# Twelve pairs of weight units as seven block products each, the memory branch moved ahead, and weight sums on VectorE

## What is computed

```python
proj = h @ w_in
(q_lat, kv_lat, k_pe, c_b, c_c, c_u, q_mem,
 g_attn, g_conv, g_mem, r) = split_cols(proj, IN_SIZES)
...
o_conv = c_b * centred_short_conv(c_c * c_u, conv_w, conv_b) * jax.nn.silu(g_conv)
...
r_attn, r_conv, r_mem = split_cols(jax.nn.sigmoid(r + b_gate), (D_MODEL, D_MODEL, D_MODEL))
y = r_attn * (o_attn @ w_br_attn) + r_conv * (o_conv @ w_br_conv) + r_mem * (o_mem @ w_br_mem)
return x + y @ w_out
```

## Time and profile before

| | |
|---|---|
| Median of 3 runs | 2596.67 us (2593.72 to 2598.73) |
| Profiled execution, first to last instruction | 2595.3 us |
| Mean granted TensorE clock | 0.986 |
| TensorE busy | 2476.7 us, 95% |
| VectorE busy | 1323.2 us, 51% |
| ScalarE busy | 762.5 us, 29% |
| GpSimd busy | 875.1 us, 34% |

### The profile page before, as it was taken

How to read it: one execution, slowest core, us unless ns; L and a number is a source line. 1 busy time by engine, 2 the same in 40 slices (tenths; PEclk the granted TensorE clock), 3 DMA queues, 4 the chain that set the end, 5 groups by cost and what they waited for, 6 DMA issues and landing times.

```text
span 2595.3 us, 33878 instructions
## 1 busy us (share of the span) xinstructions
PE 2476.7 (95%) x13700; PEld 2026.8 (78%) x13700; DVE 1323.2 (51%) x1338; ACT 762.5 (29%) x1166; POOL 875.1 (34%) x383
## 2 busy tenths in 40 slices
PE   6999888899999999999999799999999999999999
PEld 3788677677888888888877588878888877878877
DVE  3799678737654444444575887731022321342341
ACT  4201267614221211211344477720000110242010
POOL 1443300043444444444433200043344334513442
PEclk9999899999999999999999899999999999999999
DMA  6111456311111111111121400011111111113112
GB/s 261 41 41 57 116 174 185 125 49 39 43 55 43 51 47 48 48 48 48 49 110 65 136 1 2 2 41 49 65 49 49 49 41 57 57 33 121 46 45 89
DMA packets 57528, 173.79 MB, mean 67 GB/s; under 512 B 5748, under 2 KB 24440, under 8 KB 55992
## 3 DMA queue, kind: packets, MB, share of 16 engines
q1 hardware_dynamic: 51712, 149.13, 17.5%
q10 hardware_dynamic: 5688, 22.81, 2.3%
HBM read 161.37 MB, written 10.56 MB: 66 GB/s over the span
## 4 chain that ended last, share of the span: by engine, by line
PE 85%; DVE 7%; ACT 3%; issue 2%; DMA 1%; POOL 1%; SPq 0%; ACTq 0%; DVEq 0%; POOLq 0%
PE region L277 25%; PE region L279 25%; PE region L278 25%; PE pv L1936 2%; PE aux L1926 2%; DVE conv L1141 1%; ACT na_prob L1025 1%; DMA x_sb<-x_t 1%; DVE na_prob L1066 1%; PE region L2218 1%; PE pv L835 1%; PE pv L985 1%; DVE q_h L1841 1%; DVE q_h L1847 1%; DVE head_scale L421 1%
## 5 line engine op out<-in xcount | busy, mean ns | idle before, releaser
L2354 POOL TENSOR_TENSOR w_hi<-w_raw,der 128x1024 fp32r<-128x1024 f32 x186 | 362.6, 1949 | 1508.8 <-PE region L279 1464.4
L277 PE MATMUL region<-h_hi,w_hi 128*128 128x512 f32 x1760 | 691.6, 393 | 13.3 <-POOL w_lo L2357 4.9
L278 PE MATMUL region<-h_lo,w_hi 128*128 128x512 f32 x1760 | 687.8, 391 | 0.0
L279 PE MATMUL region<-h_hi,w_lo 128*128 128x512 f32 x1760 | 687.5, 391 | 0.0
L2357 POOL TENSOR_TENSOR w_lo<-w_raw,w_hi 128x1024 fp32r<-128x1024 f32 x186 | 505.0, 2715 | 14.6
L277 PEld LDWEIGHTS region<-h_hi,w_hi 128*128 128x128 f32 x1760 | 332.3, 189 | 91.8 <-issue 9.8
L279 PEld LDWEIGHTS region<-h_hi,w_lo 128*128 128x128 f32 x1760 | 332.1, 189 | 69.8
L278 PEld LDWEIGHTS region<-h_lo,w_hi 128*128 128x128 f32 x1760 | 332.3, 189 | 68.0
L277 PE MATMUL region<-ff_hi,w_hi 128*128 128x512 f32 x512 | 199.2, 389 | 0.0
L278 PE MATMUL region<-ff_lo,w_hi 128*128 128x512 f32 x512 | 199.2, 389 | 0.0
L279 PE MATMUL region<-ff_hi,w_lo 128*128 128x512 f32 x512 | 199.2, 389 | 0.0
(11 more groups left out here) (358 smaller groups left out, 3807.0 us busy)
## 6 DMA issues: line engine op xcount, KB each, us to landing
w_raw<-units SPq DMA_DIRECT2D x186, 512.0 KB, 3.3
w_raw<-w_ada_late SPq DMA_DIRECT2D x32, 512.0 KB, 4.3
bias<-na_bias SPq DMA_DIRECT2D x24, 384.0 KB, 3.7
...
head_wide<-v_spill SPq DMA_DIRECT2D x16, 512.0 KB, 3.8
...
x<-x_t ACTq DMA_DIRECT2D x1, 4096.0 KB, 14.8
```

Of the source, the lines that this page charges most:

```text
L277: pe.matmul(dst, wh, xh, start=first, stop=False)
L278: pe.matmul(dst, wh, xl, start=False, stop=False)
L279: return pe.matmul(dst, wl, xh, start=False, stop=last)
L2354: pool.tensor_tensor(w_hi[:, s], w_raw[:, s], one_col.broadcast_to([P, 1024]), ALU.mult)\
```

## The change

**Seven products.** Two units (a pair) are the rows of a 2 x 2 block matrix: a11 and a12 are the first and second half of the inputs of one tile of outputs, a21 and a22 of the other. The tokens' halves and the inputs' halves make the 2 x 2 blocks of `h2` (near is tokens 0 to 511, far the rest). Eight block products of 12 matmuls become seven (Strassen in Winograd's form), each with its own 512-wide chunk of weights: a11, a21+a22-a11, a21, a11-a21, a12, a12-(a21+a22-a11), a22. The pairs are the 16 units of `cv` and the two gates of each group of `br1`. Four chunk slots lie in `w_hi` and `w_lo`. ScalarE now writes a chunk's high part (`highs_act`), GpSimd its low part (`chunks_pool`), VectorE the four sums of weights (`sums_dve`) and five sums of results in PSUM (`pair_dve`). Three banks serve a pair, so product 4 (j == 3) waits for the first sum of results.

**Blocks of h2.** Three combinations of blocks are stored beside `h2` (`far_dve`, `far_act`, behind each group of `br0`), and `last_far_dve` writes a fourth in place over `h2`'s far half once branch 0 has read it.

**Order.** The memory stages and branch 2 come directly behind `mla`, then `gattn`, branch 0, `cv`, branch 1, `out2`. The memory rows' squares are added up on GpSimd and summed by one matmul; the memory heads are four queries and then four keys. `x3` is loaded behind branch 1's last pair and scaled during `out2`, whose units GpSimd splits from the last `chunk_done` on.

```diff
-               ("uq", 4), ("uk", 3), ("uv", 1), ("gattn", 4), ("br0", 12), ("cv", 16), ("br1", 12),
-               ("mkq", 8), ("mv", 4), ("gmem", 4), ("br2", 12), ("out2", 8)]
+               ("uq", 4), ("uk", 3), ("uv", 1), ("mkq", 8), ("mv", 4), ("gmem", 4), ("br2", 12),
+               ("gattn", 4), ("br0", 12), ("cv", 16), ("br1", 12), ("out2", 8)]
...
+    def far_dve(e, ch, k):
+        near, far = slice(0, HALF), slice(HALF, T)
+
+        def whole(slot, kk, t):
+            ch(e.tensor_tensor(far_f32[:, slot], h2_hi[:, kk, t].bitcast(F32), h2_lo[:, kk, t].bitcast(F32), ALU.add))
+
+        def made(slot, a, b):
+            e.tensor_tensor(far_f32[:, slot], far_f32[:, a], far_f32[:, b], ALU.subtract).then_inc(sem("far_made"), 1)
+
+        whole(0, k, far)
+        whole(1, k, near)
+        made(1, 0, 1)
+        whole(2, 4 + k, far)
+        made(0, 2, 0)
+        reach(e, "far_made", 3 * k + 2)
+        made(2, 2, 1)
+        for n, (which, slot) in enumerate(FAR_ORDER):
+            reach(e, "far_hi", 3 * k + n + 1)
+            e.tensor_tensor(far_lo[which][:, k], far_f32[:, slot], far_hi[which][:, k].bitcast(F32), ALU.subtract)\
+                .then_inc(sem("far_lo"), 1)
+        reach(e, "far_lo", 3 * k + 3)
...
+    def last_far_dve(e, ch):
+        near, far = slice(0, HALF), slice(HALF, T)
+
+        def low(k):
+            reach(e, "far_hi", 12 + k + 1)
+            e.tensor_tensor(h2_lo[:, k, far], far_f32[:, 2 * (k % 2)], h2_hi[:, k, far].bitcast(F32), ALU.subtract)\
+                .then_inc(sem("far_lo"), 1)
+
+        e.wait_ge(unit_done, UNIT0["br0"] + 11)
+        for k in range(4):
+            a = 2 * (k % 2)
+            if k >= 2:
+                reach(e, "far_lo", 12 + k - 1)
+            ch(e.tensor_tensor(far_f32[:, a], h2_hi[:, 4 + k, near].bitcast(F32), h2_lo[:, 4 + k, near].bitcast(F32), ALU.add))
+            ch(e.tensor_tensor(far_f32[:, a + 1], far_hi[1][:, k].bitcast(F32), far_lo[1][:, k].bitcast(F32), ALU.add))
+            e.tensor_tensor(far_f32[:, a], far_f32[:, a], far_f32[:, a + 1], ALU.subtract).then_inc(sem("far_made"), 1)
+            if k:
+                low(k - 1)
+        low(3)
+        reach(e, "far_lo", 16)
...
+    SIDES = [(h2_hi[:, 0:4, near_x], h2_lo[:, 0:4, near_x]), (far_hi[1], far_lo[1]), (far_hi[0], far_lo[0]), (far_hi[2], far_lo[2]),
+             (h2_hi[:, 4:8, near_x], h2_lo[:, 4:8, near_x]), (h2_hi[:, 4:8, far_x], h2_lo[:, 4:8, far_x]),
+             (h2_hi[:, 0:4, far_x], h2_lo[:, 0:4, far_x])]
+    BANK = [0, 1, 2, 1, 0, 2, 1]
+
+    def pair_pe(e, pair):
+        for j in range(7):
+            e.wait_ge(chunk_ready, pair.done(j))
+            if j == 0 and pair.before is not None:
+                e.wait_ge(second_sum, pairs[pair.before].summed(5))
+                e.wait_ge(near_end, pair.before + 1)
+            if j == 3:
+                e.wait_ge(second_sum, pair.summed(1))
+            if j == 4:
+                e.wait_ge(first_copy, pair.n + 1)
+            if j == 5:
+                e.wait_ge(second_sum, pair.summed(3))
+            if j == 6:
+                e.wait_ge(second_sum, pair.summed(2))
+            at, s, cols = chunk_of(pair.c + j)
+            wh, wl = w_hi[at, s, cols], w_lo[at, s, cols]
+            xh, xl = SIDES[j]
+            dst = pair.banks[BANK[j]]
+            for k in range(4):
+                w = slice(k * P, k * P + P)
+                e.matmul(dst, wh[:, w], xh[:, k], start=(j < 3 and k == 0), stop=False, skip_group_check=True)
+                e.matmul(dst, wh[:, w], xl[:, k], start=False, stop=False, skip_group_check=True)
+                last = e.matmul(dst, wl[:, w], xh[:, k], start=False, stop=(k == 3), skip_group_check=True)
+            last.then_inc(chunk_done, 1)
+
+    def part_pe(e, pos, c):
...
+        def high(upto):
+            while high.next < min(upto, N_CHUNKS):
+                c = next(at)
+                high.next = c + 1
+                src, step, u = sources[c]
+                if c < 4:
+                    e.wait_ge(unit_done, UNIT0["cv"] - 1 + c // 2)
                 else:
...
+                    e.wait_ge(chunk_done, c - 3)
+                e.wait_ge(raw_loaded[u % 2], 16 * (u // 2 + 1))
+                if step:
+                    reach(e, "w_sum", step)
+                copy(e, w_hi[chunk_of(c)], src).then_inc(sem("chunk_hi"), 1)
...
+    def chunks_pool(e):
+        def low(c, src):
+            reach(e, "chunk_hi", c + 1)
+            e.tensor_tensor(w_lo[chunk_of(c)], src, w_hi[chunk_of(c)].bitcast(F32), ALU.subtract).then_inc(chunk_ready, 1)
...
+            low(c, a11)
+            reach(e, "w_sum", n + 3)
+            low(c + 1, a11)
+            low(c + 2, a21)
+            reach(e, "w_sum", n + 4)
+            low(c + 3, w_diff[:])
+            low(c + 4, a12)
+            low(c + 5, a11)
+            freed(c + 5)
+            low(c + 6, a22)
+            freed(c + 6)
...
+        if i == 0:
+            e.wait_ge(raw_loaded[s], 16 * (pair.unit // 2 + 1))
+            e.wait_ge(raw_loaded[1 - s], 16 * ((pair.unit + 1) // 2 + 1))
+            if pair.n:
+                e.wait_ge(chunk_ready, pairs[pair.n - 1].done(3))
+            combine(1, w_diff[:], a11, a21, ALU.subtract)
+            combine(2, a21, a21, a22, ALU.add)
+        elif i == 1:
+            e.wait_ge(chunk_ready, c + 1)
+            combine(3, a11, a21, a11, ALU.subtract)
+        else:
+            e.wait_ge(chunk_ready, c + 2)
+            combine(4, a11, a12, a11, ALU.subtract)
...
+        a, b, c = pair.banks
+        e.wait_ge(first_copy, pair.n + 1)
+        e.wait_ge(chunk_done, pair.done(1))
+        add(1, second_t, first_copy_t, b)
+        e.wait_ge(chunk_done, pair.done(3))
+        add(2, third_t, first_copy_t, b)
+        far_far(lambda dst: add(3, dst, third_t, c))
+        if ahead:
+            sums_dve(e, ahead, 0)
+        e.wait_ge(chunk_done, pair.done(5))
+        near_far(lambda dst: add(4, dst, second_t, c))
+        if ahead:
+            sums_dve(e, ahead, 1)
+        e.wait_ge(chunk_done, pair.done(6))
+        far_near(lambda dst: add(5, dst, first_copy_t, b))
+        if ahead:
+            sums_dve(e, ahead, 2)
...
+        reach(e, "far_lo", 16)
+        for n in range(8):
+            if n == 1:
+                wait_region(e, pos.use)
+                wait_region(e, pos.use + 1)
+            pair_pe(e, pairs[n])
...
+    def last_branch_dve(e, pos, ch):
+        for p in range(4):
+            pair = pairs[8 + p]
+            if p:
+                reach(e, "br1_used", 2 * p)
+                for i in range(3):
+                    sums_dve(e, pair, i)
+            pair_dve(e, pair, lambda add: add(tmp[:, 1, far_t]), lambda add: add(tmp[:, 1, near_t]),
+                     lambda add: add(tmp[:, 0, far_t]))
+            for dd in range(2):
+                use, d = pos.next_use(), 2 * p + dd
+                e.wait_ge(near_end, pair.n + 1)
+                reach(e, "gate_half", 3 * p + 2 + dd)
+                e.wait_ge(chunk_done, parts[p] + dd + 1)
+                e.tensor_tensor(tmp[:, dd], region[:, use % 2], tmp[:, dd], ALU.mult).then_inc(free[use % 2], 1)
+                e.wait_ge(free[use % 2], use // 2 + 1)
+                e.tensor_tensor(y[:, d], y[:, d], tmp[:, dd], ALU.add).then_inc(sem("br1_used"), 1)
...
+            split_range(UNIT0["mkq"], UNIT0["cv"])
+            chunks_pool(pool)
+            pool.wait_ge(chunk_done, N_CHUNKS)
+            split_range(UNIT0["out2"], N_UNITS, CHUNK_UNITS)
...
+            branch_dve(dve, pos, ch, 0, behind=lambda p: far_dve(dve, ch, p))
+            last_far_dve(dve, ch)
+            for i in range(3):
+                sums_dve(dve, pairs[0], i)
+            meet(dve, pos, 3)
+            cv_dve(dve, pos, ch)
+            meet(dve, pos, 3)
+            last_branch_dve(dve, pos, ch)
             out2_dve(dve, pos, ch)
 
...
+            mem_sums_pe(pe)
+            tell()
+            mem_heads.pe(pe, pos, meanwhile=lambda: mv_pe(pe, pos))
+            tell()
+            ended(3)
+            mem_att.pe(pe, pos)
+            tell()
+            reach(pe, "ma_stored", MH * TT)
+            gate_pe(pe, pos, "gm", "gmem", o_mem)
+            tell()
+            branch_pe(pe, pos, 2, "gm_lo")
```

More of the change, by code:

```diff
@@ L2100, in branch_act, with branch_dve @@
             pos.next_use(), pos.next_use()
-    def branch_dve(e, pos, ch, b, ahead=None):
+            if behind:
+                behind(p)
+    def branch_dve(e, pos, ch, b, first=False, behind=None):
         u0 = UNIT0[f"br{b}"]
@@ new lines, in far_act @@
+    def far_act(e, k):
+        for n, (which, slot) in enumerate(FAR_ORDER):
+            reach(e, "far_made", 3 * k + n + 1)
+            copy(e, far_hi[which][:, k], far_f32[:, slot]).then_inc(sem("far_hi"), 1)
+    def last_far_dve(e, ch):
[16 more added lines that the diff above has]
+        reach(e, "far_lo", 16)
@@ new lines, in part_pe @@
+    def part_pe(e, pos, c):
+        use = pos.next_use()
```

(35 more changed lines are left out.)

364 lines of the change are left out of this document (237 added, 127 removed).

## The result

| | before | changed |
|---|---|---|
| median of 4 runs each | 2596.94 us | **2630.23 us** |
| lowest to highest | 2593.72 to 2598.73 | 2626.49 to 2632.28 |
| span of the profiled execution | 2595.3 | 2628.0 |
| mean granted clock | 0.986 | 0.975 |

The changed kernel is slower: ratio 1.0124 [1.011, 1.0137], 33 us. I had forecast 2618, in a range of 2597 to 2636.

A forecast was written before the change was run, and what follows sets the result against it. TensorE, busy 95% of the span, was taken as the bound. Costs of 65.4 us against savings of 44.2 gave +21.2, so 2618 us from a median of 2596.67; own range 2606 to 2629, overall 2597 to 2636.

The forecast's parts named there:

- five drops: +8.5: After long new TensorE waits: five falls to the 1.2 GHz level, about 1.7 us each, +8.5 us (1.7 to 17).
- Rival 1: Every wait over 2 us brings a clock drop, twelve or more: +21 instead of 8.5, about 2631 us; chance 0.15.
- Rival 4: Products don't run at 0.2266 us per matmul, so half of the 32.6 us saving goes: about 2634 us; chance 0.08.
- Start of the convolution: Before the first convolution product: TensorE waits uncovered for VectorE's sums, then the first chunks' copy and low part: +24.4 us.
- Fourth products: In each convolution pair: TensorE waits for VectorE's sum of products 1 and 2, delayed by GpSimd's low parts: +12.9 us (0 to 17).
- Rival 2: VectorE and GpSimd don't block each other at 512 columns; convolution waits fall to 0: about 2590 us, faster; chance 0.10.
- Branch 1: Second product, three times: weight sums written behind the previous group's last product and sum make TensorE wait 4.3 us each, +12.8.
- Output projection: At its start: GpSimd's first splits wait for the last chunk_done, so TensorE waits 9.3 us instead of 2.5, +6.8.
- Column sums: Memory-row sums leave branch 1 with their wait and lower clock, returning as GpSimd work and one matmul: -8.6 us.
- Memory branch: Memory heads with queries first: a 1.95 us wait and its clock drop go, 85 us for 88.6: -3 (-7 to +2).
- Weight loads are no part of it: At the convolution's fourth products: loads take 3.3 us to land, in slots freed five products ahead, and cause no wait.
- Rival 3: Unseen cover at the convolution's start, fourth products and memory stage leaves +4 us, about 2601, no change; chance 0.07.

The follow-up runs named there:

- Experiment 1: Changed kernel, with matmuls that feed nothing filling seven waits, before four fourth products of the convolution and three second products of branch 1: 2616.5 us.
- experiment 6: Changed kernel, with the weight sums of branch 1's next pair ahead of the group's last two products and sums on VectorE: 2609.6 us.
- experiment 5: Changed kernel, with far_dve's groups behind branch 0's first two groups, and last_far_dve and the first weight sums before VectorE waits for the last gates: 2612.0 us.
- experiment 2: Changed kernel, with GpSimd's low part of each chunk covering only 8 of its 512 columns: 2596.3 us.
- experiment 4: Changed kernel, with the convolution's three tap instructions on VectorE moved behind the next pair's sum of products 1 and 2: 2609.8 us.
- experiment 7: Changed kernel, with GpSimd splitting the output projection's first unit two chunks before the last, and its second unit after the last chunk: 2625.7 us.
- experiment 8: Changed kernel with four edits together: taps later, block sums ahead, branch 1's weight sums ahead, first output-projection split ahead: 2567.9 us.
- the order alone: Changed kernel's stage order and memory squares on GpSimd, but convolution, branch 1 and output projection as in the kernel before: 2587.6 us.

## Why the prediction was right, and where it was off

The direction held, and so did the mechanism of each large wait; the size (+21.2 forecast, +32.7 in the span) was off, by one term above all, the clock. That it is nearly the clock alone is luck: the other terms missed by up to 3.6 us either way (-3.4 at the start, -3.6 at the output projection, +1.7 and +1.9 in the convolution, +1.6 in the memory branch, +0.7 at the column sums, +1.5 not counted) and cancel to 0.5.

- **The clock: the term that was mis-sized.** I counted "five drops: +8.5". There were nine, one behind each wait of 3.2 us or more, and 1.7 to 2.9 us each: 19.5, beyond the 17 that I had given as its bound. I had priced every drop at one short stretch of 1.7 and left out of the count the fourth products, whose wait I had at 2.1 to 2.7. Rival 1 (2631, chance 0.15) comes nearest, +21 for 19.5, though with twelve drops where there were nine, some of them longer; my own range of 2606 to 2629 ended 1 us short. Experiment 1 shows the price by itself.
- **Seven products, -32.6.** Held: 144 matmuls fewer, and in experiment 6 100 us of branch 1 hold 443, or 0.226 us each. Rival 4 (stride broken) is out.
- **Start of the convolution, 24.4 forecast, 21.05 measured.** VectorE's work behind the last matmul of branch 0 (product and sum of its last tile, then the block sums) began at 2185.65 and the first low part at 2205.18: 19.5 us of work and 1.3 of low part.

```profile
2185.65 1.22 DVE L2124 TENSOR_TENSOR tmp<-region,tmp 128x1024 f32<-128x1024 f32 x1 [2.93 <-PE region L286]
```

```profile
2205.18 1.26 POOL L2304 TENSOR_TENSOR w_lo<-w_raw,w_hi 128x512 fp32r<-128x512 f32 x1 [36.79 <-ACT w_hi L280]
```

  The 1.0 for waits on ScalarE did not show, the 25 block sums took 17.2 us where I had 18.0, and the second chunk was hidden by the slow clock (experiment 5).
- **Fourth products, 12.9 forecast, 14.6 measured:** 12.9 at the four long ones, for which I had 10.1, and 1.7 at the others for 2.8. The releaser, the place and the blocking held (experiments 2 and 4). Missing was that the weight sum itself waits until GpSimd has read the raw half: the 0.84 in its row, which would make 3.2 of 2.1 to 2.7. The Trainium skill ("SBUF — State Buffer", section "SBUF: two separate sides") says that of a GpSimd instruction and a VectorE one with two SBUF inputs (or in a two-port mode) the one that starts first keeps the shared ports for the whole instruction. The rows agree: the low part at 2232.86 kept its 1.29 us, and the multiply beside it took 1.88 for 0.81 (the profile has the multiply begin 0.04 us earlier, but its times on GpSimd are rough). Rival 2, no blocking, is out by the same rows.
- **Branch 1, 12.8 forecast, 12.9 measured**, three times 4.29 for 4.3. Experiment 6 shows that only the place of the weight sums made it.
- **Output projection, 6.8 forecast, 3.2 measured.** Too high by 3.6: the first split there took 2.01 + 3.21 us, 0.9 over the parts alone where I had allowed 2.4, and the second, 2.88 + 3.26 us, brought no wait, on a TensorE that was itself 2.0 us slower there. Behind it stood the y_lo wait of 2.70 that experiment 7 uncovered.
- **Column sums, -8.6 forecast, -7.9 measured**: the one matmul that is left and its hand-over took 0.96 us, where I had allowed 0.3. **Memory branch, -3 forecast, -1.4 measured**, inside its bounds: the wait of 1.95 us ahead of the q head is gone, but one of 2.04 came at the norm of the last key head. The waits at the memory values (1.83) and at the scores (2.19) had been there before (1.84 and 2.19). The changed kernel, the one matmul of the column sums first:

```profile
1701.64 0.70 PE L2541 MATMUL aux<-mem_sum,ones 128*128 128x256 f32 x2
...
1771.26 1.20 PE L1758 MATMUL aux<-tmp,ones 128*128 128x256 f32 x2 [2.04 <-ACT tmp L1819]
...
1781.11 0.35 PE L2557 MATMUL region<-w_hi,hm_hi 128*128 128x256 f32 x1 [1.83 <-POOL w_lo L2710]
...
1792.67 1.22 PE L2571 MATMUL region<-m_k,q_mem 128*128 128x256 f32 x2 [2.19 <-ACTq L867]
```

  and the kernel before:

```profile
2271.00 0.35 PE L2204 MATMUL region<-w_hi,hm_hi 128*128 128x256 f32 x1 [1.84 <-POOL w_lo L2357]
...
2284.92 1.22 PE L2218 MATMUL region<-m_k,q_mem 128*128 128x256 f32 x2 [2.19 <-ACTq L860]
```

- **"Weight loads are no part of it"** was wrong. I had the slot freed five products ahead and 3.3 us to land. In the trace it is freed by the last low part of a pair, 8 us or three products ahead of the next pair, and the load takes 4.0 to 4.3. So VectorE waits 2.49 to 3.16 us for it ahead of each of the four long waits, and the chain that ended last runs through it. One of them, in the view of that chain, then on VectorE and TensorE:

```profile
2265.93 4.03 DMA w_raw<-units
```

```profile
2270.15 1.78 DVE L2346 TENSOR_TENSOR w_diff<-w_raw 128x512 f32<-128x512 f32 x1 [3.06 <-DMA w_raw<-units]
```

```profile
2277.06 0.50 PE L2248 MATMUL region<-far_hi,w_hi 128*128 128x512 f32 x1 [0.61 <-POOL w_lo L2304]
```

  This is the 1.9 us at second products, which the sum did not have. Over the traces of the changed kernel and of experiments 1 and 4 to 8, VectorE waited 2.85 to 3.99 us for a load 23 times, and each time TensorE's next second product waited 2.44 to 2.47 us less than that (0.41 to 1.52). In experiment 2 the loads were at most 1.03 late and no second product of the convolution waited. Experiment 8 still has 4.3 us of such waits. No run moved the loads alone, so their share in the fourth products' waits stays open.
- **Rival 3** (a cover that I don't see) is out: no term was under half of its forecast by being covered, except the output projection.

Seen together: the seven products are worth what they save, 32.6 us, and cost 73 (21.05, 14.6, 1.9, 12.9, 3.2 and 19.5), nearly all by the place of side work on other engines. Placed elsewhere, as in experiment 8, the same arithmetic runs at 2567.9, 19.7 under the order alone.
